# GpSimd's weight splits of a one-core inference step, issued in pieces of 512 columns

## The reference, cut to what matters

```python
def swiglu(x, w13, w2):
    gate, up = jnp.split(x @ w13, 2, axis=-1)
    return (jax.nn.silu(gate) * up) @ w2
# experts: gates holds the two normalised probabilities of a token, 0 elsewhere
for e in range(N_EXPERTS):
    out = out + gates[:, e:e + 1] * swiglu(t, w13[e], w2[e])
```

## Time and profile before

| | us |
|---|---|
| median of 3 runs (3227.09 to 3236.4) | 3233.14 |
| the profiled execution | 3229.3 |
| its span | 3227.5 |
| PE busy | 2811.4 |
| DVE busy | 1396.4 |
| POOL busy | 1217.3 |
| ACT busy | 903.5 |

### The profile page before, as it was taken

One profiled execution on the slowest core, in us unless ns is written; L12 is line 12 of the kernel. 1 busy time (PEld: TensorE's weight loads), 2 busy tenths in 40 slices (PEclk: granted clock), 3 DMA queues, 4 the chain that ended last, 5 costly groups with the idle time before them and its releaser, 6 DMA issues.

```text
span 3227.5 us, 44777 instructions
## 1 busy us (share of the span) xinstructions
PE 2811.4 (87%) x17208; PEld 2527.3 (78%) x17208; DVE 1396.4 (43%) x1856; ACT 903.5 (28%) x1355; POOL 1217.3 (38%) x432
## 2 busy tenths in 40 slices
PE   7699988888888888879999998967689999999994
PEld 3499977777777777778999998966578888778883
DVE  0400055465465465443211223244165555565655
ACT  0200023233223223212101101001155555545553
POOL 1265220220220121344646645532245545554541
PEclk9799875786786786788999998988589999999997
DMA  9333121011011011011212211210267777776674
GB/s 296 105 114 127 59 62 49 24 59 42 16 58 42 19 56 55 28 39 52 88 50 78 87 50 64 78 55 18 76 191 207 216 206 209 201 206 196 190 208 158
DMA packets 434176, 333.48 MB, mean 103 GB/s; under 512 B 16113, under 2 KB 393802, under 8 KB 433482
## 3 DMA queue, kind: packets, MB, share of 16 engines
q1 hardware_dynamic: 415258, 291.21, 30.8%
q10 hardware_dynamic: 13904, 25.69, 2.3%
q0 software_dynamic: 4960, 15.84, 1.6%
HBM read 307.98 MB, written 24.72 MB: 103 GB/s over the span
## 4 chain that ended last, share of the span: by engine, by line
PE 57%; DVE 15%; ACT 7%; issue 4%; DMA 1%; POOL 0%; DVEq 0%; SPq 0%; ACTq 0%; POOLq 0%
PE psum L609 23%; PE psum L831 9%; PE psum L592 8%; DVE m_prod L1670 4%; PE psum L751 2%; PE psum L768 2%; ACT m_hi L1156 2%; PE psum L743 2%; PE psum L758 2%; DVE m_lo L414 2%; PE psum L813 2%; PE psum L657 2%; PE psum L774 1%; DVE m_sum L1665 1%; DVE cy L1329 1%
## 5 line engine op out<-in xcount | busy, mean ns | idle before, releaser
L414 POOL TENSOR_TENSOR m_lo<-m_raw,m_hi 128x2048 fp32r<-128x2048 f32 (+1 forms) x90 | 399.3, 4440 | 400.1 <-ACT m_hi L1156 400.1
L813 PE MATMUL psum<-he,m_hi 128*128 128x384 f32 x1584 | 475.3, 371 | 54.0 <-DVE m_sum L1665 42.9
L455 POOL TENSOR_TENSOR w_hi<-raw,zero 128x2048 fp32r<-128x2048 f32 (+2 forms) x68 | 249.2, 3664 | 646.9 <-PE psum L609 547.3
L609 PE MATMUL psum<-a_hi,w_hi 128*128 128x320 f32 x1728 | 398.1, 312 | 42.8 <-DVE cy L1546 17.1
L491 POOL TENSOR_TENSOR ml<-lt,level 128x640 f32<-128x640 f32 x80 | 123.8, 1554 | 790.6 <-PE psum L592 790.6
L815 PE MATMUL psum<-he,m_lo 128*128 128x192 f32 x1584 | 404.4, 255 | 0.0
L609 PE MATMUL psum<-a_lo,w_hi 128*128 128x320 f32 x1728 | 397.6, 311 | 0.0
L609 PE MATMUL psum<-a_hi,w_lo 128*128 128x320 f32 x1728 | 396.8, 311 | 0.0
L813 PEld LDWEIGHTS psum<-he,m_hi 128*128 128x128 f32 x1584 | 306.9, 194 | 62.9 <-DVE m_sum L1665 50.6
L458 POOL TENSOR_TENSOR w_lo<-raw,w_hi 128x2048 fp32r<-128x2048 f32 (+2 forms) x68 | 333.4, 4903 | 5.3
L1156 ACT ACTIVATE m_hi<-m_raw 128x2048 fp32r<-128x2048 f32 (+1 forms) x183 | 293.1, 1611 | 133.5 <-PE psum L831 96.2
(11 more groups left out here) (298 smaller groups left out, 4611.4 us busy)
## 6 DMA issues: line engine op xcount, KB each, us to landing
m_raw<-in_moe_w_dram SPq DMA_DIRECT2D x234, 512.0 KB, 5.3
m_raw<-in_moe_w_dram SPq DMA_DIRECT2D x126, 256.0 KB, 2.8
raw<-in_mod_w_dram SPq DMA_DIRECT2D x48, 512.0 KB, 4.0
raw<-in_ffn_w_dram SPq DMA_DIRECT2D x44, 512.0 KB, 4.6
mod_raw<-in_mod_w_dram SPq DMA_DIRECT2D x16, 1024.0 KB, 6.3
raw<-in_dn_w_in_dram SPq DMA_DIRECT2D x32, 512.0 KB, 4.6
raw<-in_sc_w_in_dram SPq DMA_DIRECT2D x24, 512.0 KB, 4.0
projected<-stage ACTq DMA_DIRECT2D x16, 640.0 KB, 3.1
```

The source lines that it names most:

```text
L414: eng.tensor_tensor(m_lo[q][:, 0:n], m_raw[q][:, 0:n], m_hi[q][:, 0:n].bitcast(F32), ALU.subtract)\
L455: pool.tensor_tensor(w_hi[s][:, 0:cols], raw[s][:, 0:cols], zero[:, :].broadcast_to([P, cols]), ALU.add)\
L609: mm = pe.matmul(psum[:, 4 * s + 2 * m + a, 0:HALF], w[:, k, m, :], v[:, k, a * HALF:(a + 1) * HALF], start=(k == 0 and n == 0), stop=(k = ...
L813: pe.matmul(psum[:, b, 0:2 * CAP], wh[:, c:c + P], he[:, k, :, :].rearrange("p v c -> p (v c)"), start=(k == 0), stop=False)
```

## The change

POOL's three kinds of weight split are each issued as several instructions of 512 columns (the last one of a unit can be shorter). The semaphore is still raised once, by the last piece. DVE's own low parts (odd j) stay one instruction.

```diff
+PIECE = 512
@@ m_low(eng, x, j)
-            eng.tensor_tensor(m_lo[q][:, 0:n], m_raw[q][:, 0:n], m_hi[q][:, 0:n].bitcast(F32), ALU.subtract)\
-            .then_inc(sem(f"m_split{j % 2}"), 1)
+            w = PIECE if j % 2 == 0 else n
+            for c in range(0, n, w):
+                ins = eng.tensor_tensor(m_lo[q][:, c:c + w], m_raw[q][:, c:c + w], m_hi[q][:, c:c + w].bitcast(F32),
+                                        ALU.subtract)
+            ins.then_inc(sem(f"m_split{j % 2}"), 1)
@@ split(u, s, cols, loaded, first=False)
-                pool.tensor_tensor(w_hi[s][:, 0:cols], raw[s][:, 0:cols], zero[:, :].broadcast_to([P, cols]), ALU.add)\
-                    .then_inc(sem("hi"), 1)
+                for c0 in range(0, cols, PIECE):
+                    c1 = min(c0 + PIECE, cols)
+                    ins = pool.tensor_tensor(w_hi[s][:, c0:c1], raw[s][:, c0:c1], zero[:, :].broadcast_to([P, c1 - c0]),
+                                             ALU.add)
+                ins.then_inc(sem("hi"), 1)
                 pool.wait_ge(sem("hi"), u + 1)
-                pool.tensor_tensor(w_lo[s][:, 0:cols], raw[s][:, 0:cols], w_hi[s][:, 0:cols].bitcast(F32),
-                                   ALU.subtract).then_inc(sem("split"), 1)
+                for c0 in range(0, cols, PIECE):
+                    c1 = min(c0 + PIECE, cols)
+                    ins = pool.tensor_tensor(w_lo[s][:, c0:c1], raw[s][:, c0:c1], w_hi[s][:, c0:c1].bitcast(F32),
+                                             ALU.subtract)
+                ins.then_inc(sem("split"), 1)
```

## The result

The changed kernel takes 3142.26 us (median of 4 runs, 3138.38 to 3146.67) where the kernel before took 3230.11 on the same chip: ratio 0.9729, 95% interval 0.9703 to 0.9756. Its profiled execution took 3138.38 us with a span of 3136.6. The span is 90.9 us shorter than before; 69.7 of them lie in the expert stage and 21.2 ahead of it.

The account below looks back on a forecast made before the run. PE was taken to stall in expert up units because `m_prod` waits for POOL's long low part, followed by slow clock. Gains of 67 us (experts) and 12 (dense), 79 off 3229.3, gave 3150, taken as 3152; range 3136 to 3194.

Parts of the forecast that it names:

- The mechanism: Expert up units: `m_prod` waits for POOL's whole low part, stalling PE; with pieces it waits 0 to 1.26 us, not 3.4.
- the dense stages: Norms, `act_lo` and convolution ahead of the experts: 12 us gained in sum, bounds 6 and 18.
- The expert stage: Nine items, 7.5 us gained in each one's eleven up units: 67 us, bounds 36 and 72.
- the second rival: PE's stall returns at the even unit's low part or the transfers; half the gain lost, 3186 us; chance 0.14.
- the down units don't gain: Down units of each item: no gain, as PE is busy there for 28.95 of 29 us at clock 1.00.
- the first norm: DVE's seven adds there end near 130.7 in place of 136.61: 5.9 us gained.
- The `act_lo` operations: Before each dense expert's down units: 1.7 us in place of 3.23, 3.0 us gained for two.
- The two later norms: Norms at 1448.42 and 1952.73: 2.8 and 2.4 us gained.
- the convolution: DVE asks for the port without pause and loses all POOL works in its window: a cost of 2 us.
- The fixed cost of a piece: Each further POOL piece costs 0.10 us, bounds 0 and 0.21, hidden beside PE.
- the cover: POOL's low part of unit 6 ends 2.5 us before PE wants it.
- The first rival: POOL keeps the port through all pieces, so odd units' `m_prod` waits as before or longer: 3244 us; chance 0.09.

Follow-up runs that it names:

- e_mprod: Kernel before, POOL's instructions long, but `m_prod` of up units 2 to 8 reads its second factor from PSUM (wrong product): 3183.04 us, ratio 0.9883.
- e_experts: Against the kernel before, only the experts' low parts are cut in pieces, dense splits stay whole: 3161.19 us, ratio 0.9809.
- e_up_only: Changed kernel, but POOL's low parts of the down units are one instruction each again: 3135.66 us, ratio 0.9724.
- e_dense: Against the kernel before, only the dense splits are cut in pieces, experts' low parts stay whole: 3209.52 us, ratio 0.9949.
- e_order: Changed kernel with POOL's low part of unit 10 put ahead of the scatter and gather: 3137.04 us, ratio 0.9718.
- e_sync: Changed kernel with a tiny POOL memset and a wait for it between the gather and unit 10's low part: 3136.48 us (one execution).
- e_sync18: Changed kernel with a memset and its wait behind each gather, and POOL's low part of unit 18 alone as one instruction: 3138.13 us, ratio 0.9723.
- e_best: Changed kernel with down units' low parts on POOL whole and unit 10's low part ahead of scatter and gather: 3136.04 us, ratio 0.9724.
- e_dve: Changed kernel with DVE's own low parts (odd units) also in pieces of 512 columns: 3164.42 us, ratio 0.981.
- e_256: Changed kernel with pieces of 256 columns in place of 512: 3170.15 us, ratio 0.9815.
- e_1024: Changed kernel with pieces of 1024 columns in place of 512: 3158.31 us, ratio 0.9774.

## Why the prediction was right, and what it mis-sized

The forecast was 3152 us, and 3142.26 were measured. The mechanism and the sign were right. The mis-sized term is that of the dense stages, and the term of the experts owes part of its agreement to luck.

**The mechanism** held in each step of the expert stage. `m_prod`'s mean is 489 ns (predicted 400 to 700), its longest 1.42 us (1.6); PE's idle time before up units with `m_sum` as releaser is gone from the stage; the up units take 50.04 us (50.1) at clock 1.00; POOL works 60.4 us more on the experts' low parts alone. `e_mprod` shows that the operands, and `e_experts` that the experts' pieces and not the dense ones, are what ends this stall. The Trainium skill's page "SBUF — State Buffer", section "Who interferes with whom", has the lock between a VectorE operation with two SBUF inputs and GpSimd; 354 against 1518 ns in one kernel agrees with it.

**The expert stage**, predicted -67 us, gave -69.7, and part of this agreement is luck. The item was put at 84.5 us and is 85.2: nearly all of the difference is PE's 0.94 us for unit 18, the only trace of the second rival. There the prediction said that the down units don't gain, and did not say that they could lose. So a usual item of 91.8 us gave 6.6 us and not 7.5. What made up for it are the three items of before that were longer by 7.5 us in sum, with the clock at 0.50 behind the transposes; the changed kernel's profiled execution has no such fall, and the forecast had taken all nine items at 92. `e_up_only` shows that such falls can come back in a kernel that never waits.

**The dense stages**, predicted -12 with bounds -6 to -18, are the mis-sized term: -21.2 in the profiled pair. Part of this is no effect of the change. PE's restart at 1378.39 (1387.02 before) is reached at 1373.70 to 1383.39 in eight kernels with 512-column dense splits (the changed one, `e_dense`, `e_up_only`, `e_order`, `e_sync`, `e_sync18`, `e_best`, `e_dve`), whose work up to there is the same, and at 1381.40 to 1387.02 in the three with long ones: means 1379.2 and 1384.6, 5.4 us apart. From that restart to the start of the expert stage there is far less scatter: 867.5 us before and 869.3 and 867.7 in the two other kernels with long dense splits, 855.0 to 855.2 in seven of the eight and 853.1 in `e_dve` (859.7 with 256 columns, 864.0 with 1024). So the change gives 12.6 us behind 1378 and some 5 to 7 ahead of it (the difference of the means; the first norm by itself, below, has 7.5), 18 to 20 in sum, at or a little over the bound; `e_dense` has 17.2 between medians.

Term by term: the first norm's adds end at 129.12 in place of 136.61, 7.5 us for the 5.9 predicted, as one add gets in ahead of them (it waited 5.10 before):

```profile
116.19 1.55 DVE L1217 TENSOR_TENSOR sq_total<-sq 128x640 f32<-128x640 f32 x1
118.60 10.52 DVE L1217 TENSOR_TENSOR sq_total<-sq_total,sq 128x640 f32<-128x640 f32 x6 [0.86 <-ACT sq L944]
```

The `act_lo` operations take 1.39 for 3.23 (predicted 1.7), and the two stretches between PE's restarts that hold them give 1.4 and 2.6 us, 4.0 for 3.0. The two later norms came out as priced, 2.8 and 2.4 us between PE's restarts. The sign was wrong at the convolution: priced at +2, it gave -1.6, and a further 2.2 us went between the next two restarts, not priced at all. Of these 1.6 are one operation, DVE's low part of the convolution's output over 5120 columns, with two SBUF inputs, for which PE waits (`a_lo`, L1558: 5.79 us from 2140.70, for 7.37 before). The argument for the convolution's +2 was that DVE asks without pause and so loses all that POOL works in its window. The convolution's operations show what fails in it:

```profile
2063.87 5.44 DVE L1339 SCALAR_TENSOR_TENSOR cy<-cu,col,cy 128x127 f32<-128x127 f32 x4
...
2074.32 2.83 DVE L1339 SCALAR_TENSOR_TENSOR cy<-cu,col,cy 128x127 f32<-128x127 f32 x4
```

Next to POOL's pieces a group of four taps costs 2.0 to 3.5 us in five places and 5.4 to 5.7 in three, where with long instructions it was 2.05 in five and 6.30, 9.57 and 9.72 in three. So DVE loses turns in more groups and less in each, and the sum is a little lower: the convolution's chain took 39.8 us for 41.7. Which taps lose a turn, and why the groups differ, was not tried.

**The fixed cost of a piece** was put at 0.10 us with bounds 0 and 0.21. Four uninterrupted pieces behind the gather take 5.00 to 5.03 where one long instruction took 4.64: 0.12 to 0.13 each for the three further ones, and `e_256` gives 0.14. It is hidden, as said; that the cover ends somewhere between 512 and 256 columns is what `e_256` shows.

**The first rival** (the port stays with POOL through all pieces) had been argued against by one place where DVE got in. It is wrong for the up units in general and right for one place in each item, the pieces behind the gather. The argument looked at pieces behind a wait and not at pieces behind a transfer's issue, though the item has both. That it costs nothing here is luck in the phase: `hid_lo` and not `m_prod` is caught, which is a matter of 1 us, as `e_dve` shows at 3.5 us an item. The Trainium skill's "GPSIMD Engine Reference", section "Instruction dispatch", says that a core starts its next instruction as soon as its own share is done. If that keeps the port taken, it fits what is seen behind the gather in most kernels and not what is seen elsewhere; the same `hid_lo` in the `e_sync` pair, 5.63 against 0.36 us, says where it bears, and the five items of `e_256` are against it even there.

## What to carry to other kernels

Where a short VectorE operation with two SBUF inputs lies on the critical path beside long GpSimd instructions, look whether it ends just after one of them; cutting them gives the stall back for about 0.13 us a piece, and the best size is where the remaining wait fits the reserve and GpSimd's own lateness still does (512 of 2048 columns was the best of three sizes here; by the ratios 256 and 1024 lose 28 and 15 us of the 88). Look also at what GpSimd did just before its pieces: behind an indirect transfer's issue they can act as one long instruction, which a memset and a wait on it ended here. And when an idle time of TensorE under 1 us is removed, read the granted clock before counting the gain.

## What the runs showed of the hardware

- GpSimd pieces directly behind an indirect transfer's issue mostly don't give way to VectorE: 5.63 us for a 0.36 us subtraction in the changed kernel, in nine of nine items. With pieces of 256 columns they kept it out in four of nine (4.24 us) and gave way in five (0.92). With a 0.11 us memset and a 0.17 us wait between, the same subtraction takes 0.36 us.
- The granted clock can fall to 0.50 for 3.4 us at the end of sixteen transposes of 128x128 though TensorE had no idle time (1.6 us an item); the same instructions in the next item may leave it at 1.00. In `e_1024` it fell there for 6.8 us in every item.
- The exclusion reaches an indirect transfer's issue: 2.58 us beside VectorE's subtraction of 2048 columns, 0.9 to 1.0 alone, at most 1.45 for the gather's issues in `e_dve`, with the subtraction in pieces.
- Splits that give VectorE more turns can still lose: with 256 columns TensorE waits 2.6 us for a GpSimd part in an up unit, in four of nine items, and 1.1 to 1.9 in the others.
- The time to the 1378 us mark scatters by 10 us between executions of the same instructions, and the 855 us behind it by 0.2 in seven of eight, with the eighth 2 us shorter. A stage is better compared from its own start than from the span's.
